# Attention scores as stacked split products, value products spread over the units, and expert tiles requested earlier

## The reference, cut to what matters

```python
# first block, one layer, l = 0
mod = jax.nn.silu(c) @ w_ada[l] + b_ada[l]            # six blocks of 1024: sh1 sc1 gt1 sh2 sc2 gt2
kv_c = hc @ w_in[l][:, 512:768]                       # 256 context tokens: keys and values
h = modulate(rmsnorm(x, g_mix[l]), sh1, sc1)
q, k, v, bg, cg, hv = jnp.split(h @ w_in[l], SPLIT_POINTS, axis=-1)
q, k = apply_rope(q, cos, sin), apply_rope(k, cos, sin)
att = windowed_attention(q, k, v, k_c, v_c, sink[l])  # 8 heads of 64, 2 KV heads; softmax over
                                                      # [sink, 256 context keys, keys with |i-j| <= 128]
conv = short_conv_mixer(bg, cg, hv, conv_w[l])
x = x + gt1 * (jnp.concatenate([att, conv], axis=-1) @ w_out[l])
h2 = modulate(rmsnorm(x, g_ffn[l]), sh2, sc2)
x = x + gt2 * expert_choice_ffn(h2, w_router[l], w_gate[l], w_up[l], w_down[l])  # 16 experts, 64 tokens each
return rmsnorm(x, g_final)
```

## Time and profile before

| | us |
|---|---|
| median of 3 runs | 2501.95 (2501.6 to 2503.89) |
| the profiled execution's own time | 2502.74 |
| its span | 2501.0 |
| input projection, first strips to last | 36.13 to 154.19 |
| attention, first mask to the start of the output projection's rest | 158.05 to 235.66 |
| output projection and router | 235.66 to 304.18 |
| experts | 304.18 to 756.08 |
| second block | 756.08 to 2501.0 |

### The profile page before, as it was taken

One profiled execution on the slowest core, in us unless ns is written; L12 is line 12 of the kernel. 1 busy time (PEld: TensorE's weight loads), 2 busy tenths in 40 slices (PEclk: granted clock), 3 DMA queues, 4 the chain that ended last, 5 costly groups with the idle time before them and its releaser, 6 DMA issues.

```text
span 2501.0 us, 29717 instructions
## 1 busy us (share of the span) xinstructions
PE 2458.6 (98%) x11265; PEld 1802.0 (72%) x11265; DVE 1132.8 (45%) x1732; ACT 735.2 (29%) x1049; POOL 49.5 (2%) x28
## 2 busy tenths in 40 slices
PE   7999999999999999999999999999999999999999
PEld 4876744434437888888888888888887667888887
DVE  6785312222227444336444334444337565544422
ACT  4245210100014333224333223333224354333321
POOL 0042000000000000000000000000000000000000
PEclk8999999999999999999999999999999999999999
DMA  7552699999992223313222322323222211223332
GB/s 309 191 168 98 262 408 421 421 420 421 421 407 89 98 94 112 102 55 110 92 100 99 104 91 84 101 92 113 96 90 68 80 43 43 93 92 101 105 104 68
DMA packets 84654, 404.29 MB, mean 162 GB/s; under 512 B 9176, under 2 KB 9560, under 8 KB 60896
## 3 DMA queue, kind: packets, MB, share of 16 engines
q1 hardware_dynamic: 84576, 403.22, 43.3%
HBM read 401.08 MB, written 2.10 MB: 161 GB/s over the span
## 4 chain that ended last, share of the span: by engine, by line
PE 92%; DVE 4%; ACT 2%; DMA 1%; issue 1%; SPq 0%; ACTq 0%; DVEq 0%
PE pair L1142 23%; PE pair L1144 23%; PE pair L1143 23%; PE pair L1438 9%; PE pair L1463 4%; PE pair L1374 2%; PE pair L1693 1%; PE pair L1831 1%; PE pair L1402 1%; PE pair L1288 1%; PE pair L1801 1%; PE pair L1802 1%; DMA ada_first<-in_w_ada 1%; PE pair L1403 1%; DMA stage<-in_gate 0%
## 5 line engine op out<-in xcount | busy, mean ns | idle before, releaser
L1856 DVE TENSOR_TENSOR wL<-stage,wH 128x1024 fp32r<-128x1024 f32 (+3 forms) x301 | 389.0, 1292 | 775.0 <-ACT wH L699 774.5
L1142 PE MATMUL pair<-hH,wH 128*128 128x512 f32 x1672 | 658.4, 394 | 8.5 <-DVE hL L1966 2.9
L1144 PE MATMUL pair<-hH,wL 128*128 128x512 f32 x1672 | 651.7, 390 | 0.0
L1143 PE MATMUL pair<-hL,wH 128*128 128x512 f32 x1672 | 651.6, 390 | 0.0
L699 ACT ACTIVATE wH<-stage 128x1024 fp32r<-128x1024 f32 (+3 forms) x301 | 335.2, 1114 | 842.1 <-PE pair L1144 842.1
L1142 PEld LDWEIGHTS pair<-hH,wH 128*128 128x128 f32 x1672 | 314.4, 188 | 80.3 <-DVE hL L1901 4.2
L1143 PEld LDWEIGHTS pair<-hL,wH 128*128 128x128 f32 x1672 | 314.5, 188 | 66.9 <-issue 2.4
L1144 PEld LDWEIGHTS pair<-hH,wL 128*128 128x128 f32 x1672 | 314.4, 188 | 65.8
L1142 PE MATMUL pair<-gH,wH 128*128 128x512 f32 x704 | 273.9, 389 | 0.0
L1143 PE MATMUL pair<-gL,wH 128*128 128x512 f32 x704 | 273.9, 389 | 0.0
L1144 PE MATMUL pair<-gH,wL 128*128 128x512 f32 x704 | 273.9, 389 | 0.0
(11 more groups left out here) (365 smaller groups left out, 2135.1 us busy)
## 6 DMA issues: line engine op xcount, KB each, us to landing
ring<-in_experts SPq DMA_DIRECT2D x182, 1024.0 KB, 19.5
stage<-in_gate SPq DMA_DIRECT2D x88, 512.0 KB, 3.2
stage<-in_up SPq DMA_DIRECT2D x88, 512.0 KB, 3.2
stage<-in_down SPq DMA_DIRECT2D x64, 704.0 KB, 4.0
adaw<-in_w_ada SPq DMA_DIRECT2D x32, 512.0 KB, 5.2
stage<-in_w_in SPq DMA_DIRECT2D x18, 512.0 KB, 3.7
ring<-in_experts SPq DMA_DIRECT2D x16, 512.0 KB, 11.4
stage<-in_mla_in SPq DMA_DIRECT2D x9, 512.0 KB, 3.3
```

Of the source, the lines that this page charges most:

```text
L1142: pe.matmul(ps, lh, rh, start=first, stop=False)
L1143: pe.matmul(ps, lh, rl, start=False, stop=False)
L1144: return pe.matmul(ps, ll, rh, start=False, stop=last)
L1856: dve.tensor_tensor(low, stage[:, n % STAGE, 0:w], high, ALU.subtract).then_inc(strip_lo, 1)
```

## The change

- Scores: keys and queries are split too. After the rotary step ACT writes the high part (`high_part`), DVE the low part (`low_half`), and SP moves them by 24 DMAs from on-chip memory to on-chip memory (`stacked`) so that high and low parts of a query head lie on top of each other in `qS`, and the key's high part twice (and its low part twice) in `kS`. A unit's scores are then two fp32r products per piece of keys; the pieces are 512 wide, 384 and 256, or 256 and 256.
- Value products: one key tile of a block per unit, beginning 11 units after the block's first, with a second pair of `PT` buffers. ACT's and DVE's step on the result moves from 12 units after the block's first to 16.
- The four convolution splits move from before the attention to the units 6, 8, 10 and 12; the last modulation vectors to behind unit 0's mask.
- Block 5 of the modulation moves from POOL to PE: eight parts of four fp32 products (32 output rows, 256 columns each) at s = 9 to 16, with eight loads of 512 KB at SP's s = 6 to 13.
- Strips are staged at 4 KB distance, which frees room; the masks come as one load at s = 12; the ring's slots are placed anew. SP requests tiles 0 to 9 and 14 in one go at the attention's end, 13 and 12 while the output strips are being split, the others (10, 11, 15, 16, 17, 19, 18) after the output strips have been used.
- Some semaphores are merged.

```diff
@@ SP
+            def stacked(r):
+                sp.wait_ge(qk_lo, r + 1)
+                for part in range(2):
+                    if r == K_AT:
+                        for j in range(2):
+                            for at in range(0, P, 64):
+                                sp.dma_start(kS[at:at + 64, j, part, :].bitcast(F32), part_k[64 * j:64 * j + 64, part, :].bitcast(F32)).then_inc(qk_moved, 16)
+                    else:
+                        for j in range(2):
+                            at = 64 * (j ^ part)
+                            sp.dma_start(qS[j][at:at + 64, ROT_Q[r], :].bitcast(F32), part_q[64 * j:64 * j + 64, part, :].bitcast(F32)).then_inc(qk_moved, 16)
             for s in range(-2, 18):
                 strip_after(s)
...
                 for t in range(ADA_TO[s], ADA_TO[s + 1]):
                     if t + 4 < 24:
                         ada(16 + t + 4)
-            for j in range(KD):
-                gate_tile(j)
+                if GATE_LOAD <= s < GATE_LOAD + KD:
+                    gate_tile(s - GATE_LOAD)
+                if s - 2 in ROT_AT:
+                    stacked(ROT_AT[s - 2])
...
+            experts(8, 0, 8)
+            experts(9, 0, 9)
+            spare_tile(0)
+            sp.wait_ge(strip_lo, W_OUT + 6)
+            experts(13, 0, 13)
             sp.wait_ge(strip_lo, FFN1A)
+            experts(12, 0, 12)
             sp.wait_ge(strip_used, FFN1A)
@@ ACT
+            def high_part(r):
+                act.wait_ge(rope_done, r + 1)
+                if r == K_AT:
+                    act.wait_ge(strip_used, V_AT + 1)
+                    ins = act.activation(part_k[:, 0, :], kT[:, :], ACT.Copy)
+                else:
+                    if r:
+                        act.wait_ge(qk_moved, 64 * r if r < K_AT else 64 * (r + 1))
+                    ins = act.activation(part_q[:, 0, :], qT[:, ROT_Q[r], :], ACT.Copy)
+                ins.then_inc(qk_hi, 1)
             for s in range(18):
                 hi(s + 2)
                 copy_out(s)
+                if s - 1 in ROT_AT:
+                    high_part(ROT_AT[s - 1])
@@ DVE, loop over s
                 lo(s + 2)
                 if s - 1 in ROT_AT:
...
+                if s - 2 in ROT_AT:
+                    low_half(ROT_AT[s - 2])
@@ PE
+            def gate_part(j):
+                pe.wait_ge(first_or_gate_landed[j % 4], 32 + 16 * (j // 4 + 1))
...
+                for g in range(4):
+                    mm = pe.matmul(pb[6][32 * g:32 * g + 32, 0:256], stat[:, j:j + 1].broadcast_to([P, 32]), gate_w[j % 4][:, 256 * g:256 * g + 256],
+                                   start=(j == 0), stop=(j == KD - 1))
+                q = qS[j][:, a, n * P:(n + 1) * P]
+                for at, key, w in key_pieces(n):
+                    pe.matmul(pair[j][:, at:at + w], q, kS[:, j, 0, key:key + w], start=True, stop=False)
+                    mm = pe.matmul(pair[j][:, at:at + w], q, kS[:, j, 1, key:key + w], start=False, stop=True)
...
+                n, k = divmod(u - LAG1 - 1 - 7, 8)
+                if 0 <= n < NB and k < len(kv_tiles[n]):
+                    att_values(n, k)
-            pe.wait_ge(ada_added, GATES)
-            pe.wait_ge(shift_copied, 1)
-            for m in range(KD):
-                mm = pe.matmul(pb[3][:, m:m + 1], gate_acc[:, m * P:(m + 1) * P], ones[:, 0:1], start=True, stop=True)
```

More of the change, by code:

```diff
@@ L163, in build @@
         wL = place("wL", [P, 2, WIDE], F32R, WL)
+        stage4 = place("stage4", [P, STAGE, KD * P], F32, ST)
+        w4H = place("w4H", [P, 2, KD * P], F32R, ST + 16 * KB)
+        w4L = place("w4L", [P, 2, KD * P], F32R, ST + 24 * KB)
         std = place("std", [P, T], F32, TM)
@@ L425, in halves, with staged @@
                 return firstH[:, n - FFN1A, :], firstL[:, n - FFN1A, :]
+            if n < FFN1A:
+                return w4H[:, n % 2, :], w4L[:, n % 2, :]
             return wH[:, n % 2, 0:width[n]], wL[:, n % 2, 0:width[n]]
+        def staged(n):
+            return stage4[:, n % STAGE, :] if n < FFN1A else stage[:, n % STAGE, 0:width[n]]
         def count(it, before, per, n):
@@ L476, in build, with key_pieces, masked_scores @@
         LAST = (PAIRS - 1) * 24
-        kv_tiles = {n: [4, 5] + list(range(keys(n)[0] // P, keys(n)[1] // P)) for n in range(NB)}
+        kv_tiles = {0: [4, 5, 0, 1], 1: [4, 5, 0, 1, 2], 2: [1, 2, 3, 4, 5], 3: [4, 5, 2, 3]}
+        def key_pieces(n):
+            return {0: [(0, 0, 512)], 1: [(128, 0, 384), (512, 384, 256)], 2: [(128, 384, 384), (512, 0, 256)],
+                    3: [(0, 0, 256), (256, 512, 256)]}[n]
+        def masked_scores(u):
+            n, a, j = UNITS[u]
+            w = C + keys(n)[1] - keys(n)[0]
+            first = key_pieces(n)[0][0]
+            return pair[j][:, first:first + w], window[:, MASK_AT[n]:MASK_AT[n] + w]
         ffns = [(FFN1A, T_FFN1A, 0, N1A), (FFN2A, T_FFN2A, 1, N2A), (FFN1B, T_FFN1B, 2, N1B), (FFN2B, T_FFN2B, 3, N2B)]
@@ L698, in hi @@
                     act.wait_ge(strip_used, shifted(n - 1, it))
-                act.activation(halves(n)[0], stage[:, n % STAGE, 0:width[n]], ACT.Copy).then_inc(strip_hi, 1)
+                act.activation(halves(n)[0], staged(n), ACT.Copy).then_inc(strip_hi, 1)
             def square(q, k, src):
@@ L1276, in att_turn, with att_values @@
                 mm.then_inc(p_turned, 1)
[L1278 to L1290 removed]
+            def att_values(n, k):
+                if k == 0:
+                    pe.wait_ge(pt_act, 8 * n + 8)
+                    pe.wait_ge(v_ready, 2)
+                    if n == 0:
+                        pe.wait_ge(mod_ready, 6)
+                    else:
+                        pe.wait_ge(att_lo, n)
+                tiles = len(kv_tiles[n])
+                v = kv_tiles[n][k]
+                for j in range(2):
+                    mm = pe.matmul(pb[7][64 * j:64 * j + 64, :], V[:, v, 64 * j:64 * j + 64], PT[n % 2][j][:, k, :],
+                                   start=(k == 0), stop=(k == tiles - 1))
+                if k == tiles - 1:
+                    mm.then_inc(pv_done, 1)
             def mixed_out(s, features):
@@ L1299, in mixed_out @@
                 return mm
-            for u in range(len(UNITS) + LAG1 + 1):
+            for u in range(len(UNITS) + LAG1 + 5):
                 if u < len(UNITS):
@@ L1853, in lo @@
                 dve.wait_ge(strip_hi, shifted(n + 1, it))
-                w = width[n]
                 high, low = halves(n)
-                dve.tensor_tensor(low, stage[:, n % STAGE, 0:w], high, ALU.subtract).then_inc(strip_lo, 1)
+                dve.tensor_tensor(low, staged(n), high, ALU.subtract).then_inc(strip_lo, 1)
             def clear(q):
@@ L2059, in att_soft @@
                 else:
-                    dve.wait_ge(window_loaded, 32)
+                    dve.wait_ge(window_loaded, 16)
                 dve.tensor_copy(prob[:, u % 4, w:w + 1], stat[:, 48 + head:49 + head])
                 dve.wait_ge(scored, u + 1)
-                dve.tensor_tensor_reduce(prob[:, u % 4, 0:w], pair[j][:, 0:w], (window if n else window_first)[:, 0:w], 1.0, -3e38,
+                scores, mask = masked_scores(u)
+                dve.tensor_tensor_reduce(prob[:, u % 4, 0:w], scores, mask, 1.0, -3e38,
                                          ALU.add, ALU.max, m2).then_inc(masked, 1)
```

243 lines of the change are left out of this document (121 added, 122 removed).

## The result

The changed kernel takes 2529.52 us (median of four runs, 2529.01 to 2531.48) against 2502.81 of the kernel before on the same chip (2501.6 to 2503.89): a ratio of 1.0108, 95% interval 1.0091 to 1.0126, 26.7 us slower. The forecast was 2515.7 with a range of 2501 to 2525. So the direction was right and the size about half. The profiled execution took 2531.48, 2.0 above the median, with a span of 2529.7 (before: 2501.0) and a mean granted clock of 0.988 (0.994). A few executions of the experiments and of the kernel before took 3081 us and more; they are left out of ranges and ratios.

The account below looks back on a forecast made before the run. PE's order was taken to limit the input projection, PE and DVE the attention, PE and DMA both nearly full among the experts. 16.6 + 2.4 + 3.2 - 7.9 - 0.5 = +13.8 us, a median of 2515.7; range 2501 to 2525.

Parts of the forecast that it names:

- step 1: Input projection: ACT's high parts wait for the previous tile's moves, so PE stalls four times, 16.6 us in sum.
- Rival A: Input projection: the moves don't hold ACT, so the stalls and clock loss go; median 2497.1; 12%.
- the length of that chain: Input projection: split, move issue at 0.43 us each, landing at 3.0, next strip; stalls of 5.0, 3.9, 2.3 and 5.4.
- Gate parts: Input projection: eight modulation parts on PE, 0.45 us each, seven of them counting: +3.2, bounds 3.2 and 12.6.
- The eight loads: nothing: Input projection: the gate parts' loads, 4.2 MB three strips ahead at 0.58 of DMA's time, cost nothing.
- Rival C: Input projection: gate parts run in twos or in turn, 3.2 to 9.4 us more, 2519 to 2525; 8%.
- Attention: First mask to output projection: PE's scores get cheaper, DVE sets the pace, splits wait; -7.9 us, bounds -15.0 and -4.
- Rival B: Attention gives its full 15 us because ACT's split falls in a gap of DVE; 2508.6; 13%.
- Experts: Expert stage: all 20 tiles landed at the start, but PE waited for none before; 0, bounds 0 and -2.5.
- step 4: Router and experts: row sums go, -0.5 us; early tiles gain 0, though the second block's first strips land sooner.
- Rival D: Expert stage is bound by DMA, so four early tiles of 2.5 us save 10 us, 2505.7; 7%.
- step 3: Attention: -7.9 us; bound -15.0 if the six splits had no waits and PE were never late.

Follow-up runs that it names:

- e1: Changed kernel with splits and moves of four of the five rotated tiles at later strips, nothing else changed: 2507.57 us.
- e2: Changed kernel with useless matmuls filling three of PE's idle stretches in the input projection: 2529.79 us.
- e9: Changed kernel with later splits, half of the moves left to the engines, and convolution low parts one unit after their high parts: 2503.70 us.
- e10: e9 with the modulation's gate block moved out of the input projection into the router: 2506.70 us.
- e3: Changed kernel with each convolution tile's low part on DVE one unit later than its high part on ACT: 2524.92 us.
- e6: e1 with seven of the eight gate tiles left out, both their loads and their products: 2505.41 us.
- e4: Changed kernel with expert tiles from the ninth on requested only when the output projection's strips are done, as before the change: 2529.58 us.
- e12: e10 with five gate tiles in other places, so nine expert tiles instead of six are requested before the output projection is done: 2497.55 us.
- e11: Changed kernel with half of the moves left to the engines and the wait for earlier moves on DVE's low part instead of ACT's high part: 2514.55 us.
- e7: e1 with a block's value products in one run after its last transposes, as before the change: 2511.68 us.

## Why the prediction was wrong, by its own steps

The differences of the table, put beside the terms: +9.7 before the first mask, +3.5 in the attention, -0.9 in the router, +2.6 behind it; together the 15 us between 2516.5 and the profiled 2531.48.

- **The mechanism of step 1 was right.** ACT's queue, its three waits for moves, PE idle four times, and each time until DVE's rotary step or low part. e1 takes it away and 22 us go. Rival A is refuted.
- **The step that failed most is the length of that chain.** It should have let PE begin strip 10 at 122.5; PE began it at 129.60, and these 7.1 are nearly half of the 15. Link by link: the three landings, 3.0 each in the chain, took 5.0, 3.8 and 4.5, together 4.3 more, and all above the 3.7 that was the dear end. The eight moves of the key tile, priced at 0.43, took 0.74, 2.5 more in all; the four of the second tile 0.60, 0.7 more. The first tile's moves were issued by 84.9, as forecast. The view that the earlier trace rows is from has a row, not shown there, that would have warned: the loads of `w_ada` on the same queue, most of them in the same stretch, took 5.2 at the median:

```profile
adaw<-in_w_ada SPq DMA_DIRECT2D x32, 512.0 KB, 5.2
```

- PE's idle times were 7.7, 2.6, 0.3 and 9.0 (19.6) instead of 5.0, 3.9, 2.3 and 5.4 (16.6). That is only 3.0 more, since PE's slow matmuls filled most of the rest of the 7.1, and e2 shows that they cost nothing there. The estimate from the Trainium skill's "DMA: Bandwidth & Descriptors", Anatomy of one DMA, was 2.3 us for a move; here the measurement decides, and with four in flight it is about double on this path.
- **Behind strip 10** the forecast has 56.0 us to the first mask and the trace 58.6, +2.6. Gate parts are 0.8 of it. The slow matmuls there lose 3.4 by their starts: 1.6 right behind the stall and 1.8 in the group without idle time ahead of it, against 2.4 forecast and well within its bounds. What is left, 0.8, falls by difference to the start of the attention, where I had a gain of 1.75.
- **Gate parts:** 0.56 for one instead of 0.45, 3.9 against 3.2. True as long as the stall stands. With it gone, the block costs 8.7 us (e9 to e10): 4.5 of products, 1.4 of PE's waits for tiles and their sum (4.1 against 2.7), and 2.8 that I can't break down. "The eight loads: nothing" holds only beside the stall. Rival C is refuted; the groups do run side by side.
- **Attention:** 62.5 us from the first mask to the first rest, 59.0 forecast. The splits cost what was said (1.01 to 1.11 of wait and 0.69 each), and e3 gave that wait back for four of the six. The step that failed is PE's unit with values, 2.05 and 1.81 (1.31 and 0.5 over it) forecast, 2.35 and 2.12 measured: values 1.01 instead of 0.89, scores 0.69 instead of 0.60, transposes 0.64 instead of 0.56. By the starts of the masks these units overrun DVE's pace by 6.1 us, where I had 2.4 (a sum that doesn't come out: its own terms, 5 x 0.54 - 1.1 and 5 x 0.5 - 1.0, make 3.1). Rival B needed the waits gone and they weren't.
- **Experts:** 0 forecast, +1.5 measured, and 1.1 more in all that follows. The stage took 451.8 to 453.5 us in nine of the other runs that touch it not at all or little, and 455.2 in e6, so a cause in the change is not shown; it stays open. Where the time went in the profiled execution can be read: PE waited 1.86 us instead of 0.42 before the first FFN product, for a strip whose load had kept ACT idle 3.02 us (1.57 before), and then the granted clock was 0.74, 0.50 and 0.90 in the three stretches of 2 us from 784 on, where it had stayed at 1.00. e4 has neither that wait nor that fall, and from its first FFN product to the end it takes 1744.6 us, against 1746.1 in the changed kernel and 1744.9 before. The forecast that these strips would land sooner (step 4) did not come true. Rival D is wrong for this change (e4), but its ground is right: e10 shows that the transfers take over if the stage starts some 8 us sooner without more tiles in place. Before the change both limits lay within a few us of each other, which "PE waited for no tile" did not show.

The range missed by 4.5 us. Its upper end, 9.3 above the forecast, held 6.4 for the chain, which took 7.1, and about 3 for the gate parts, and had nothing for the attention (3.5) and for what stands behind the router (2.6). Even the 6.4 came by a slip: 18.7 and three more make 21.7 and not 23. The -15.0 as the bound of step 3 doesn't follow from its terms either (7.9, six waits of 1.09 and the 2.4 make 16.8); nothing measured here hangs on it.

## What to carry to other kernels

A wait put into the queue of an engine that also feeds the main line costs the whole loop behind it (split, issue, landing, split), once a round; price each link at the dearest row of the same stretch, not a middle one (here the loads of 5.2 us and not the 3.0), and place the step where the loop has already closed. Where the waits are taken away, look at the next limit before counting the gain: here 22 us came back from four changed positions, 4.6 from one unit's delay, and 9.8 at the experts' start were worth only 1.7 until nine tiles instead of six were asked for early. In these kernels requests ahead of time were worth nothing to a stage that started late (e4) and several us to one that started early (e12).

## What the runs showed of the hardware that was not expected

In the changed kernel a move of 128 KB between partitions, issued by SP, took 0.60 to 0.77 us to issue, and the last of four had landed 3.8 to 5.0 us after its issue where ACT waited for it; moves of 192 KB took 0.74 and 4.5. The size alone doesn't set the issue time: moves of 192 KB took 0.60 each in e11 (2.39 us for four) and 0.97 in e7 (7.74 for eight). The granted clock fell to 1.2 GHz in the attention after PE had been busy 2.27 of 4 us, and it fell in e1 between 110 and 120 us behind a gate part and the small matmuls of a sum, without any idle time in the trace. The sum alone, in the kernel before, in e6 and in e12, left it at 1.00, but so did both together in e7 and e9. Keeping the clock up by added matmuls worked in e2 and bought nothing, since PE was not what the stage waited for.
